# First mixer of a hybrid decoder: score levels of the two head groups in two chains two levels apart, 64 moving queries a block, every weight split on VectorE

## What is computed

```python
# one input projection feeds two head groups
# A (HGRN2): 4 heads, dk 128      B (GLA): 4 heads, dk 64
f = lb + (1 - lb) * sigmoid(a_f);  k_A = 1 - f;  log_g_A = log(f)
z = b_low @ w_up + b_up;           log_g_B = log_sigmoid(z) / 16
# both: S_t = diag(exp(log_g_t)) S_(t-1) + k_t v_t^T ;  o_t = S_t^T q_t
# so with b = cumsum(log_g):
#   scores[t, s] = sum_d q[t, d] k[s, d] exp(b[t, d] - b[s, d])   for s <= t
# then o = scores @ v, a norm for each head, times silu(gate), output projection
```

## Time and profile before

| | |
|---|---|
| median of 3 runs | 1212.5 us (1210.69 to 1213.33) |
| the profiled execution | 1214.44 us, of which the span of the trace is 1212.6 us |
| PE busy | 892.2 us (74%) |
| DVE busy | 369.5 us (30%) |
| ACT busy | 303.6 us (25%) |
| POOL busy | 45.2 us (4%) |
| HBM traffic | 441.15 MB read, 365 GB/s over the span |
| mean granted PE clock | 0.934 of 2.4 GHz |

### The profile page before, as it was taken

The page is one execution under the profiler, slowest core; times in us unless marked ns, Lnnn a source line. Parts: engine busy times, 40 slices in busy tenths (PEclk is TensorE's granted clock), DMA queues, the critical chain, the costliest instruction groups (busy, mean ns, idle before and its releaser), DMA issues.

```text
span 1212.6 us, 25066 instructions
## 1 busy us (share of the span) xinstructions
PE 892.2 (74%) x10181; PEld 546.2 (45%) x10186; DVE 369.5 (30%) x837; ACT 303.6 (25%) x512; POOL 45.2 (4%) x22
## 2 busy tenths in 40 slices
PE   8997897777666667666668999777666666667674
PEld 6976773443333333333336986434333333333332
DVE  5799763111111111111115785111111111111112
ACT  4643534111111011011004764121111110110102
POOL 2054100000000000000000000000000000000000
PEclk9999799999888988889899999999999888999888
DMA  9633177999999999999996469799999999999994
GB/s 340 241 121 138 36 310 291 428 430 428 429 429 428 430 427 430 427 430 428 429 418 232 156 249 397 328 428 430 428 429 428 429 429 428 429 428 429 427 429 204
DMA packets 44818, 442.69 MB, mean 365 GB/s; under 512 B 3616, under 2 KB 4784, under 8 KB 20080
## 3 DMA queue, kind: packets, MB, share of 16 engines
q1 hardware_dynamic: 44368, 440.90, 87.2%
q10 hardware_dynamic: 288, 1.05, 0.2%
q0 software_dynamic: 128, 0.26, 0.1%
HBM read 441.15 MB, written 1.05 MB: 365 GB/s over the span
## 4 chain that ended last, share of the span: by engine, by line
DMA 50%; PE 30%; DVE 12%; ACT 4%; issue 3%; SPq 1%; DVEq 0%; ACTq 0%
DMA weights<-in_moe_w_dram 50%; PE bank L922 12%; PE bank L594 3%; PE bank L596 3%; PE bank L595 3%; PE bank L931 3%; DVE weights L1425 2%; PE bank L940 2%; PE bank L906 1%; DVE weights L1402 1%; DVE weights L1416 1%; ACT weights L975 1%; DVE w_lo L1288 1%; PE bank L677 1%; ACT w_hi L1033 1%
## 5 line engine op out<-in xcount | busy, mean ns | idle before, releaser
L922 PE MATMUL bank<-weights,gates 128*32 128x256 f32 x4096 | 289.1, 445 | 136.0 <-DMA weights<-in_moe_w_dram 125.9
L922 PEld LDWEIGHTS bank<-weights,gates 128*32 128x32 f32 x4096 | 148.0, 127 | 261.5 <-DMA weights<-in_moe_w_dram 125.2
L931 PE MATMUL bank<-weights,gates 128*32 128x256 f32 x2048 | 123.8, 382 | 85.9 <-DVE gates L1627 60.7
L1625 DVE TENSOR_TENSOR gates<-gates,bank 128x128 f32<-128x128 f32 x64 | 18.4, 287 | 419.7 <-ACT gates L975 419.7
L931 PEld LDWEIGHTS bank<-weights,gates 128*32 128x32 f32 x2048 | 62.8, 109 | 146.9 <-issue 87.1
L975 ACT ACTIVATE gates<-bank 128x128 f32<-128x128 f32 (+1 forms) x68 | 19.9, 296 | 413.5 <-PE bank L922 412.9
L1621 DVE TENSOR_TENSOR gates<-bank,vecs 128x256 f32<-128x256 f32 x64 | 27.2, 424 | 266.1 <-PE bank L915 266.1
L940 PE MATMUL bank<-gates 32*128 32x256 f32 x1024 | 73.3, 400 | 31.2 <-ACT gates L1185 31.2
L906 PE MATMUL bank<-tok,gates 128*32 128x256 f32 x1024 | 68.5, 385 | 15.9 <-issue 10.2
L940 PEld LDWEIGHTS bank<-gates 32*128 32x128 f32 x1024 | 46.2, 184 | 63.4 <-ACT gates L1185 62.0
L1185 ACT COPY gates<-bank 128x256 f32<-128x256 f32 x64 | 23.8, 372 | 191.5 <-PE bank L931 191.5
(11 more groups left out here) (212 smaller groups left out, 1018.2 us busy)
## 6 DMA issues: line engine op xcount, KB each, us to landing
weights<-in_moe_w_dram SPq DMA_DIRECT2D x192, 2048.0 KB, 35.2
weights<-in_even_w_in_dram SPq DMA_DIRECT2D x6, 2048.0 KB, 13.5
weights<-in_odd_w_in_dram SPq DMA_DIRECT2D x5, 2048.0 KB, 21.7
weights<-in_even_w_in_dram SPq DMA_DIRECT2D x2, 1024.0 KB, 10.0
weights<-in_even_w_out_dram SPq DMA_DIRECT2D x1, 2048.0 KB, 8.8
weights<-in_even_w_out_dram SPq DMA_DIRECT2D x2, 1024.0 KB, 4.8
weights<-in_odd_w_out_dram SPq DMA_DIRECT2D x1, 2048.0 KB, 7.5
weights<-in_odd_w_out_dram SPq DMA_DIRECT2D x2, 1024.0 KB, 5.5
```

Of the source, the lines that this page charges most:

```text
L922: ins = pe.matmul(bank[6][PASS * j:PASS * (j + 1), 0:T], got_T[:, k % 2, k // 2, :], up[:, k, :, j * P:(j + 1) * P], start=(k == 0), stop= ...
L931: ins = pe.matmul(bank[7][PASS * q:PASS * (q + 1), T:2 * T], hid_T[:, c, :], down[:, c, q * T:(q + 1) * T], start=(c == 0), stop=(c == Q - 1),
```

## The change

1. The score levels of A and B become two chains with semaphores of their own (`gap_ready_A`, `gap_ready_B` and so on). In loop step i the engines work at level i of A and level i - `LAG` = i - 2 of B. A's first two levels come ahead of the loop: `scores_A(0)` ahead of step 7's matmuls, `scores_A(1)` behind them.
2. The moving operand of a level's matmul is the second halves of the blocks alone, 64 columns and not 128. The keep reads 64 scores a block: one instruction of 512 elements for A (before two of 512), two of 256 for B (before two of 512). Level 0 and the cross block stay at 128 columns.
3. Banks: A uses bank 0 or 2 by the level's parity, B banks 1 and 3 or 6 and 7. Projections keep 4 and 5.
4. The rests of steps 9 to 15 move from POOL to DVE, one in each loop step.
5. `softplus` and the two `fold`s move behind the rest of step 16, ahead of the head norms. The log of f (ACT) and the running sum of A (DVE) come earlier.
6. `heads` is cut in two: `heads(0)` waits for A alone, then the cross block of B, then `heads(1)`.
7. B's running sum has a restart table of its own, which POOL sets at the start.

```diff
-PROJECT_AT = (0, 1, 2, 3, 4, 5, 7)
+LAG = 2
-POOL_STEPS = (range(9, 16), ())
@@ gpsimd
+            pool.memset(restart_B, 1.0).then_inc(restart_B_set, 1)
...
-                for i in POOL_STEPS[l]:
-                    pool.tensor_tensor(lo, raw_w, hi.bitcast(F32), ALU.subtract).then_inc(lo_set_pool.sem, 1)
@@ tensor
-                for i in range(len(LEVELS) + 2):
-                    if i in PROJECT_AT:
-                        project(8 + PROJECT_AT.index(i))
-                    scores(i)
+                def second_halves(v, h):
+                    return v.rearrange("p (n c) -> p n c", c=2 * h)[:, :, h:]
...
+                                part, at = buf[:, h, a * P:(a + 1) * P], (a * HEADS + h) * 64
+                                ins = pe.matmul(bank[0 if i % 2 else 2][:, at:at + 64], part, second_halves(part, LEVELS[i - 1]),
+                                                start=True, stop=True)
...
+                scores_A(0)
+                by_channel(0, 7, range(4, 8))
+                scores_A(1)
+                for i in range(2, len(LEVELS) + 2):
+                    project(6 + i)
+                    scores_A(i)
+                    scores_B(i - LAG)
+                scores_B(len(LEVELS) + 1 - LAG + 1)
...
+                heads(0)
+                scores_B(len(LEVELS) + 1)
...
+                heads(1)
@@ scalar
+                exp_A(2)
                 round_step(0, 9)
+                for i in range(3, len(LEVELS) + 2):
+                    exp_A(i)
+                    exp_B(i - LAG)
+                    round_step(0, 7 + i)
+                    if i % 2:
+                        keep((i - 3) // 2)
+                exp_B(len(LEVELS) + 1 - LAG + 1)
+                act.wait_ge(scores_ready_A, 3 + len(LEVELS))
+                act.copy(SA[:, 1024:1536], bank[2][:, :]).then_inc(cross_kept_A, 1)
+                exp_B(len(LEVELS) + 1)
...
+                    act.copy(dst, src).then_inc(cross_kept_B, 1)
                 round_step(0, 16)
@@ vector
-                    rest_step(0, i)
-                softplus()
-                for l in range(2):
-                    fold(l)
...
+                for i in range(3, len(LEVELS) + 2):
+                    gap_A(i)
+                    gap_B(i - LAG)
+                    keep_A(i - 2)
+                    decay_A(i)
+                    if i - LAG == 1:
+                        dve.wait_ge(bqk_kept, 4)
+                    if i - LAG >= 2:
+                        keep_B(i - LAG - 2)
+                    decay_B(i - LAG)
+                    rest_step(0, 7 + i)
+                keep_A(len(LEVELS))
+                gap_B(7)
+                keep_B(5)
+                decay_B(7)
+                gap_B(8)
+                keep_B(6)
+                decay_B(8)
+                keep_B(7)
                 rest_step(0, 16)
+                softplus()
+                for l in range(2):
+                    fold(l)
```

More of the change, by code:

```diff
@@ L744, in scores, with scores_B @@
+                    ins.then_inc(scores_ready_A, 1)
+                def scores_B(i):
+                    buf = decB[i % 2].rearrange("p (m t) -> p m t", m=2)
+                    keys, queries = buf, buf
+                    if i == 0:
+                        keys, queries = (z.rearrange("p (m t) -> p m t", m=2) for z in (kB, qB))
                         pe.wait_ge(bqk_kept, 4)
@@ L746, in scores @@
                     else:
-                        pe.wait_ge(decayed, 4 * (i - 1) + 2)
+                        pe.wait_ge(decayed_B, 2 * i)
                     if i > 1:
-                        pe.wait_ge(scores_kept, 4 * (i - 2) + 2)
+                        pe.wait_ge(scores_kept_B, 2 * (i - 1))
                     cross = i == len(LEVELS) + 1
                     tiles = (0,) if cross else range(TT)
[L752 to L763, removed]
                     for a in tiles:
@@ L1044, in even_mixer, with exp_level, exp_A, exp_B @@
                     act.copy(qA[:, m * T:(m + 1) * T], bank[4 + m][:, 0:T]).then_inc(aq_kept, 1)
+                round_step(0, 7)
                 act.wait_ge(*step_done.at(0, 5))
                 act.copy(low, bank[0][0:16, 0:T]).then_inc(low_kept, 1)
-                round_step(0, 7)
-                act.wait_ge(f_ready, 4)
-                f(decA[0], kA, ACT.Ln).then_inc(f_logged, 1)
+                def exp_level(i, buf, b_run, ready, done):
+                    h = (LEVELS + (P,))[i - 1]
+                    act.wait_ge(ready, i)
+                    v = buf.rearrange("p (n c) -> p n c", c=2 * h)
+                    if h == P:
+                        first, scale_first = v[:, :, 0:h], 1.0
+                        second = b_run.rearrange("p (n c) -> p n c", c=2 * h)[:, :, h:]
+                    else:
+                        first, scale_first, second = v[:, :, 0:h], -1.0, v[:, :, h:]
+                    f(v[:, :, h:], second, ACT.Exp).then_inc(done, 1)
+                    f(v[:, :, 0:h], first, ACT.Exp, scale=scale_first).then_inc(done, 1)
+                def exp_A(i):
+                    exp_level(i, decA[i % 2], bA, gap_ready_A, gap_exped_A)
+                def exp_B(i):
+                    exp_level(i, decB[i % 2], bB, gap_ready_B, gap_exped_B)
+                def keep(g):
+                    act.wait_ge(*step_done.at(0, 9 + 2 * g))
+                    dst, at = ((tok, 0), (tok, 512), (gates, 0))[g]
+                    for a in range(TT):
+                        act.copy(dst[:, a, at:at + 512], bank[4 + a][:, :]).then_inc(proj_kept.sem, 1)
+                exp_A(1)
                 round_step(0, 8)
@@ L1356, in even_mixer @@
             def even_mixer():
-                for i in (3, 4):
-                    rest_step(0, i)
+                rest_step(0, 3)
                 dve.wait_ge(sig_done, 4)
@@ new lines, in even_mixer, with gap @@
+                rest_step(0, 6)
+                def gap(i, buf, b_run, read, count, ready):
+                    h = (LEVELS + (P,))[i - 1]
+                    if i >= 3:
+                        dve.wait_ge(read, count)
+                    v, bv = (z.rearrange("p (n c) -> p n c", c=2 * h) for z in (buf, b_run))
+                    n = v.shape[1]
+                    border = bv[:, :, h - 1:h]
+                    if h == P:
+                        ins = tt(v[:, :, 0:h], border.to_broadcast([P, n, h]), bv[:, :, 0:h], ALU.subtract)
+                    else:
+                        ins = tt(v, bv, border.to_broadcast([P, n, 2 * h]), ALU.subtract)
+                    ins.then_inc(ready, 1)
@@ new lines, in decay, with gap_A @@
+                def decay(i, buf, k_, q_, exped, done):
+                    h = (LEVELS + (P,))[i - 1]
+                    v, kv, qv = (z.rearrange("p (n c) -> p n c", c=2 * h) for z in (buf, k_, q_))
+                    dve.wait_ge(exped, 2 * i)
+                    tt(v[:, :, h:], v[:, :, h:], qv[:, :, h:], ALU.mult).then_inc(done, 1)
+                    tt(v[:, :, 0:h], v[:, :, 0:h], kv[:, :, 0:h], ALU.mult).then_inc(done, 1)
+                def gap_A(i):
+                    gap(i, decA[i % 2], bA, scores_ready_A, i, gap_ready_A)
@@ new lines, in keep_A @@
+                def keep_A(i):
+                    if i == 0:
+                        for a in range(TT):
+                            dve.wait_ge(scores_ready_A, a + 1)
+                            keep(0, SA[:, a * 512:(a + 1) * 512], bank[2 + a], scores_kept_A)
+                        return
+                    dve.wait_ge(scores_ready_A, 2 + i)
+                    dve.wait_ge(scores_kept_A, 1 + i)
+                    if i == 1:
+                        dve.wait_ge(masks_set, 1)
+                    keep(i, SA[:, 0:1024], bank[0 if i % 2 else 2], scores_kept_A)
@@ L1373, in even_mixer, with keep_B @@
+                def keep_B(i):
+                    for q in range(2):
+                        dve.wait_ge(scores_ready_B, 2 * i + q + 1)
+                        if i:
+                            dve.wait_ge(scores_kept_B, 2 * (i - 1) + q + 1)
+                        keep(i, SBp[q], bank[(1, 3)[q] if i % 2 else 6 + q], scores_kept_B)
+                gap_A(1)
+                dve.wait_ge(aq_kept, 4)
+                decay_A(1)
+                rest_step(0, 7)
                 dve.wait_ge(z_ready, 1)
```

162 lines of the change are left out of this document (81 added, 81 removed).

## The result

The changed kernel takes 1202.15 us (median of 6 runs, 1196.82 to 1204.87) beside 1212.91 for the kernel before (6 runs, 1209.43 to 1214.8): a ratio of 0.990, 95% interval 0.9883 to 0.9917. That is 10.8 us by the medians and 12.1 by the ratio. 1200.5 was forecast, with 12 us of gain.

The account below looks back on a forecast made before the run. DVE, stalled beside POOL's splits, was taken to pace the levels, with PE the bound afterwards. Along PE 14.4 us earlier, less 2.1 for the half clock, gave about 12 us gain: 1200.5 us, range 1198.5 to 1203.5.

Parts of the forecast that it names:

- The stall: Score levels: DVE stands still during POOL's two-input splits, some 4.4 us each, seven some 30 us.
- DVE's step: Loop step on DVE after the change: gaps, keeps, decays and split sum to 7.6 us.
- A's copy: A's keep on DVE in a loop step: one instruction of 512 elements, 0.7 us where two took 1.34.
- PE's step and 64 columns: Loop step on PE: projection 5.6, A's scores 1.76, B's 1.0, together 8.4 us; 64 columns save little.
- The router's rows with 32 columns: Nearest traced fp32 matmuls, pairs 0.25 us apart, as slow an instruction as with 128 columns; used to price 64 columns.
- The first rival: Score matmuls on PE: 64 columns do save time, a loop step is DVE's 7.6 us, time 1196; 12 in 100.
- The sum: Along PE from z to heads(0) at 120.2, then the tail to the gate products' end at 140.0, 14.4 us earlier.
- softplus and folds: Tail, behind the rest of step 16 and ahead of the head norms: 5.2 us on DVE that nothing covers.
- The half clock: PE after its pause to 140: clock at 0.50 for some 4.3 us, costing 2.1 us; bounds nothing or 3.8.
- Not passed on: Rival, behind the mixer: the gain stops at a transfer, first experts' loads ending the wait; 1212.5 us, 4 in 100.
- the clock falling in the levels: Rival, PE in the levels: each 4.3 us stretch at 0.50 costs 2.1 us, time over 1214; 4 in 100.
- an old price of the keeps: Rival, DVE's keeps in the loop or missed hand-overs: step 8.8 us, 3 to 5 us less gain, 1203.5 to 1206; 25 in 100.

Follow-up runs that it names:

- splits_only: Kernel before, with only the rests of steps 9 to 15 moved from POOL to DVE: 1204.51 us, ratio 0.9909.
- splits_on_pool: Changed kernel with the rests of steps 9 to 15 back on POOL: 1216.62 us, ratio 1.0018 to the kernel before.
- scores_twice: Changed kernel with each score matmul of A's levels 1 to 7 issued twice: 1214.52 us, ratio 1.0005 to the kernel before.
- warm_wait: Changed kernel with 40 matmuls of zeros on PE in its wait for group A's y: 1201.38 us, ratio 0.9885 to the kernel before.
- keeps_twice: Changed kernel with every masked copy of levels 1 to 7 made twice: 1211.93 us, ratio 0.9993 to the kernel before.
- round16_first: softplus_in_wait plus ACT's round of step 16 ahead of the copies of B's cross block: 1197.41 us, ratio 0.9868 to the kernel before.
- softplus_in_wait: Changed kernel with softplus and the two folds moved into DVE's wait ahead of A's second decay: 1198.91 us, ratio 0.9874 to the kernel before.
- changed_again: Changed kernel as it is, run again beside some of the experiments: 1205.09 us, ratio 0.9925 to the kernel before.

## Why the prediction was right, point by point

**The stall.** DVE stands still beside POOL's splits: shown by splits_only (11.1 us gained by moving them alone; in the kernel before PE never waits for POOL in the levels, so what was gained is DVE's time) and by the rows of splits_on_pool, where the long instructions come back. Its 13.4 us are lost in part to POOL's own late results. The Trainium skill, "GPSIMD Engine Reference", section "1. Specifications", has VectorE and GpSimd share their SBUF interfaces, with contention for VectorE instructions with two SBUF inputs or in a 2-port mode. The traces agree on the first kind: the long ones are products and gaps, which have both inputs in SBUF. In splits_on_pool there is also a tensor_scalar of 4.74 us with one input; whether it is in a 2-port mode no run shows. The size isn't in that section: nearly the whole of POOL's instruction. And what reads a score bank, in PSUM, keeps its time, as here in the kernel before, where two products with the identity take 1.27 us within POOL's split:

```profile
69.09 4.88 POOL L572 TENSOR_TENSOR w_lo<-weights,w_hi 128x2048 fp32r<-128x2048 f32 x1 [3.18 <-ACT w_hi L1033]
69.45 1.27 DVE L1400 TENSOR_TENSOR weights<-bank,consts 128x512 f32<-128x512 f32 x2
```

**DVE's step.** 7.6 forecast, 7.17 measured; products, gaps and split at the prices of rows 3 and 6. The overlaps between instructions were counted too small. One term was taken too low: A's copy, put at 0.7, is 0.73 up to level 5 and 1.30 for levels 6 and 7.

**PE's step and 64 columns.** 8.4 forecast, 8.43 measured. A's scores took 1.82 us (1.76 forecast), B's 1.04. The router's rows with 32 columns were the right neighbour. By the Trainium skill, "TensorE: Matmul & The Clock Gate", section "LDWEIGHTS (loading the stationary operand)", a weight load costs its columns divided by 1.2 in ns, which gave an estimate of 1.71 us for A. The trace agrees within 6% (1.82); the router's pairs, at 0.125 us an instruction, lie farther off. For B's pieces on 64 rows the same estimate would be too long: their instructions follow each other 0.065 us apart. The first rival, that streaming counts, is out. scores_twice shows that PE is the bound of the loop.

**The sum.** Counted from z at 50.64 in the kernel before, heads(0) was put at 120.2, 69.6 us on; it came 69.8 on. y of group A was to come 14.4 us earlier. From z to its end was 103.8 us and is 89.3 (48.51 to 137.79): 14.5.

**softplus and folds.** 5.2 us uncovered was the estimate; taking them out brought y 4.2 us forward, the rest being held by ACT's squares (DVE waits 0.56 and 1.01 us for them, where it waited 0 and 0.76), and the stage 4.7.

**The half clock.** 2.1 us forecast from rows 9; 2.3 measured, as the gain of warm_wait.

**Not passed on, the clock falling in the levels.** Neither happened. Against the kernel before, SP's first load that waits for an expert comes at 190.49 and not 204.75; less the 2.1 us by which the z mark differs, that is 12.1 us, the same as at the end of step 15. Behind this point the 12.1 us can't be told from the 7 us by which executions differ. The clock was 1.00 throughout the levels.

**What went another way than I thought.** I had listed an old price of the keeps at 3 to 5 us, by a step longer than PE's. keeps_twice shows that a longer DVE step isn't paid in the loop at all: it shortens DVE's lead, and what is missing at the end of the loop is paid in one wait and the slow clock behind it. The sum was right, but here with luck. It followed PE, and the only wait that it checked was the one for the rest of step 9, with 0.5 us of room; it took all later ones to have more. In fact DVE comes to B's level 7 some 0.25 us after PE. No term of the sum says so; a DVE path 2 us longer up to that place would have made the gain about 2 us smaller.

What stays open: how much the two chains give by themselves. splits_only has neither chains nor halves and is 1.0 us behind. That number hides two larger ones: counted from z, PE ends heads and starts step 15 at 88.5 us in splits_only and at 76.8 in the changed kernel, 11.7 us earlier, and the new tail takes 10.7 of them back, 4.7 for softplus and the folds and 2.3 for the half clock; the other 3.7 have no experiment of their own but the 0.9 of round16_first. With softplus out of the tail (softplus_in_wait) the distance to splits_only is 5.7 us, which chains, halves and the early log share. They weren't taken apart. It isn't PE's step: that is 8.54 us in splits_only (98.09 less 89.55) and 8.43 here. What splits_only has and the changed kernel hardly has are waits of PE for DVE in the last levels, 5.9 us in all, and the slow clock behind them.

## What to carry to other kernels

An instruction that takes ten times as long as its twin is probably waiting: look at what another engine does in the same microseconds before counting it as work. Moving 34 us of POOL's work onto the busiest engine of this stage made the kernel faster. In a loop with several engines, the lead of the one that isn't the bound is an account: a longer step draws on it without any wait, and the bill comes behind the last step, so look at the waits there. A sum along the bound engine alone doesn't show this; add up the second engine to the last meeting point too. Work moved out of a loop must go where its engine waits, not where the next stage starts.

## What the runs showed of the hardware

- fp32 matmuls with a stationary tile of 128x128 take as long with 64 moving columns as with 128: 0.114 us an instruction (1.82 / 16) against 0.117. On 64 rows each, B's took 1.04 against 1.09 for 16.
- A masked copy of 512 elements took 0.72 us with runs of 4 elements and more, and 1.30 with runs of 2 or 1; 256 elements 0.4 and 0.65. A product of 512 took 0.68 to 0.73 in all levels.
- A tensor_scalar of 128x512 without a second tensor, 0.43 us alone, took 4.74 beside POOL's split.
- Executions of one kernel differ by clock events. In the changed kernel PE starts the first projection at 16.68 us after a pause of 2.03, with the clock at 1.00; in changed_again after 2.76, and the clock is at 0.50 from 20 to 22 us. The z mark then stands at 50.81 and not 48.51, 2.3 us later, 0.8 of it by the later start (17.50). Windows of 2 us of the one and the other:

```profile
20.00:22.00 2.00, 2.00 (x19) 2.00 (x18) 1.44 (x9) 0.25 (x2) 0.00 (x0) 1.00 1.09 352
```

```profile
20.00:22.00 2.00, 2.00 (x12) 2.00 (x11) 1.62 (x6) 0.21 (x1) 0.00 (x0) 0.50 1.10 347
```
